# Up layers that run on unnormalised x, with 1/rms put in at the relu, and square sums moved to GpSimd

## The reference

```python
def rms_norm(x, g):
    xf = x.astype(jnp.float32)
    y = xf * lax.rsqrt(jnp.mean(xf * xf, axis=-1, keepdims=True) + NORM_EPS)
    return (y * g.astype(jnp.float32)).astype(x.dtype)

...
        x = x + jnp.concatenate([o_mix, o_mem], axis=-1) @ p['w_out'][i]
        h = rms_norm(x, p['norm_ffn_g'][i])
        x = x + jnp.square(jax.nn.relu(h @ p['w_up'][i])) @ p['w_down'][i]
    y = rms_norm(x, p['final_norm_g'])
```

## Time and profile before

| | us |
|---|---|
| median of 3 runs | 2136.28 |
| lowest, highest | 2129.35, 2141.01 |
| profiled execution | 2138.74 |
| its span | 2137.0 |
| TensorE busy | 2010.4 (94%) |
| VectorE busy | 1004.9 (47%) |
| ScalarE busy | 460.6 (22%) |
| GpSimd busy | 15.8 (1%) |
| mean granted clock of TensorE | 0.956 |

### The profile page before, as it was taken

The page is one execution under the profiler, slowest core; times in us unless marked ns, Lnnn a source line. Parts: engine busy times, 40 slices in busy tenths (PEclk is TensorE's granted clock), DMA queues, the critical chain, the costliest instruction groups (busy, mean ns, idle before and its releaser), DMA issues.

```text
span 2137.0 us, 26562 instructions
## 1 busy us (share of the span) xinstructions
PE 2010.4 (94%) x10334; PEld 1625.0 (76%) x10334; DVE 1004.9 (47%) x2078; ACT 460.6 (22%) x1179; POOL 15.8 (1%) x32
## 2 busy tenths in 40 slices
PE   8999888999979899999999999999989899999996
PEld 6888555677757788888887888788876688888885
DVE  3110799545554445355433424066545444445443
ACT  2211666333221111100001512233341111100000
POOL 0000000000000000000000000000000000000000
PEclk9999999999979899999999989999998999999998
DMA  5442100455522122222223111200001122222211
GB/s 217 165 150 73 40 1 1 139 178 177 158 79 79 60 79 79 79 79 89 89 72 150 60 40 60 82 32 1 31 28 60 59 79 79 81 89 87 79 60 42
DMA packets 60287, 175.41 MB, mean 82 GB/s; under 512 B 6529, under 2 KB 39442, under 8 KB 46850
## 3 DMA queue, kind: packets, MB, share of 16 engines
q1 hardware_dynamic: 56898, 160.77, 22.4%
q0 software_dynamic: 3264, 12.93, 1.5%
HBM read 160.75 MB, written 12.93 MB: 81 GB/s over the span
## 4 chain that ended last, share of the span: by engine, by line
PE 89%; DVE 6%; ACT 3%; issue 1%; DMA 0%; POOL 0%; SPq 0%; DVEq 0%; POOLq 0%; ACTq 0%
PE psum L1720 43%; PE psum L1704 15%; PE psum L842 5%; PE psum L1253 5%; PE psum L1686 2%; PE psum L915 2%; PE psum L698 2%; PE psum L679 1%; PE psum L875 1%; PE psum L1858 1%; PE psum L662 1%; DVE sbuf L1587 1%; DVE sbuf L789 1%; ACT sbuf L740 1%; PE psum L583 1%
## 5 line engine op out<-in xcount | busy, mean ns | idle before, releaser
L1720 PE MATMUL psum<-sbuf 128*128 128x272 f32 x4032 | 938.5, 395 | 24.6 <-DVE sbuf L2063 20.2
L1720 PEld LDWEIGHTS psum<-sbuf 128*128 128x128 f32 x4032 | 767.7, 191 | 193.6 <-DVE sbuf L2063 21.1
L1704 PE MATMUL psum<-sbuf 128*128 128x272 f32 x1344 | 329.4, 405 | 5.3 <-DVE sbuf L2063 5.3
L1704 PEld LDWEIGHTS psum<-sbuf 128*128 128x128 f32 x1344 | 261.1, 196 | 64.4 <-issue 6.7
L1923 ACT ACTIVATE sbuf<-sbuf 128x544 f32<-128x544 f32 x40 | 25.7, 655 | 545.0 <-DVE sbuf L2145 386.0
L1253 PE MATMUL psum<-sbuf 128*128 128x128 f32 (+3 forms) x1020 | 124.7, 278 | 12.4 <-DVE sbuf L1571 5.2
L1253 PEld LDWEIGHTS psum<-sbuf 128*128 128x128 f32 (+3 forms) x1020 | 117.6, 190 | 19.4 <-DVE sbuf L1571 6.0
L842 PE MATMUL psum<-sbuf 128*128 128x256 f32 x448 | 107.9, 392 | 0.0
L842 PEld LDWEIGHTS psum<-sbuf 128*128 128x128 f32 x448 | 82.0, 188 | 17.5 <-issue 1.2
L2074 DVE TENSOR_TENSOR sbuf<-sbuf 128x512 f32<-128x512 f32 x72 | 49.8, 691 | 86.8 <-PE psum L1720 86.7
L1948 ACT ACTIVATE sbuf<-psum 128x544 f32<-128x544 f32 x42 | 26.2, 623 | 293.2 <-PE psum L1704 293.2
(11 more groups left out here) (365 smaller groups left out, 2061.3 us busy)
## 6 DMA issues: line engine op xcount, KB each, us to landing
sbuf<-in_w SPq DMA_DIRECT2D x100, 1024.0 KB, 4.8
sbuf<-in_pages SPq DMA_DIRECT2D x256, 128.0 KB, 2.4
sbuf<-in_mcache SPq DMA_DIRECT2D x2, 4096.0 KB, 15.7
sbuf<-in_win SPq DMA_DIRECT2D x8, 512.0 KB, 4.6
out_win_o<-sbuf POOLq DMA_DIRECT2D x8, 512.0 KB, 2.9
sbuf<-in_state SPq DMA_DIRECT2D x6, 512.0 KB, 6.0
out_state_s<-sbuf POOLq DMA_DIRECT2D x6, 512.0 KB, 3.0
sbuf<-in_x SPq DMA_DIRECT2D x1, 2176.0 KB, 11.8
```

Of the source, the lines that this page charges most:

```text
L1704: last = mm(both(t % 2)[:, half, :], lhs, halves_of(rhs(k))[:, half, :], start=k == 0, stop=k == KT - 1)
L1720: ins = mm(to, lhs(k), rhs(k), start=first and k == 0, stop=last_ and k == 3, skip_group_check=True)
```

## The change

1. **Up on unnormalised x.** ScalarE copies x times the gain into a new buffer `xg`, block by block as VectorE finishes the blocks of each out unit (`gained`); up multiplies `xg`. The factor 1/rms is the same for all channels of a token, so it is put in after the product: VectorE's step is now max(c, 0) * rstd, and ScalarE squares the result. `xg` takes the place of the last 8 tiles of `u`, which move to `hT`.
2. **Squares.** ScalarE squares tile 0 into `sq_sum`, and GpSimd adds tiles 1 to 6 to it. TensorE sums only `sq_sum` and tile 7 (`norm_sums`): 4 matmuls for a norm instead of 16. For norms 1 and 3 they stand behind the first up unit, and the root and the reciprocal beside the second.
3. **Pairs.** The scheme now pairs tile 2k with 2k + 1 (before: k with k + 4), so the input sums of up can be made a pair at a time beside the out units (`gain_sums`).
4. **Order in a unit**: products 1, 5, 6, 2, 7, 3, 4 (before 1, 2, 6, 5, 7, 3, 4). The first unit of each out has 1, 2, 5, 6, 7, 3, 4.
5. **Heads of out.** For out0 the sums over the columns without samples, over the memory tiles, and the weight sums are made before the last sample is read. For out1 the weight sums are made before the last reciprocal of the mixer. TensorE no longer waits for the last read.
6. **Stores** of the result are issued by SyncE. Several semaphores are joined, and SyncE waits for norm 2's sums before it loads four tables of layer 1.

```diff
-        u = view(sbuf[:, pj0 + 8192 - FFT * TT_:pj0 + 8192], FFT, TT_)
+        u0 = pj0 + 8192 - FFT * TT_
+        u_low = view(sbuf[:, u0:u0 + 24 * TT_], 24, TT_)
+        xg = view(sbuf[:, u0 + 24 * TT_:u0 + FFT * TT_], KT, TT_)
+        u_at = lambda t, n: u_low[:, t:t + n, :] if t < 24 else hT[:, t - 24:t - 24 + n, :]
...
+        LATE, EARLY = (1, 5, 6, 2, 7, 3, 4), (1, 2, 5, 6, 7, 3, 4)
...
+                    sp.wait_ge(sq_used, KT + 2)
                     sp.dma_start(mkv[1], mem_out[1]).then_inc(in_mkv1, 16)
...
+            for k in range(KT):
+                sp.wait_ge(h_ready, 2 * KT + k + 1)
+                sp.dma_start(y_out[:, k, :], hT[:, k, :]).then_inc(y_stored, 16)
...
+            def add_squares(n):
+                for k in range(1, KT - 1):
+                    pool.wait_ge(sq_ready, n * KT + k + 1)
+                    if k > 1:
+                        pool.wait_ge(sq_added, 6 * (n - 1) + k - 1)
+                    pool.tensor_tensor(sq_sum, sq_sum, sq[:, k % 2, :], ALU.add).then_inc(sq_added, 1)
...
+            before_last()
             dve.wait_ge(cn_std, 2)
             dve.reciprocal(rinv[0:TS, 4, :], rinv[0:TS, 4, :]).then_inc(cn_rec, 1)
...
+            def norm_sums(n):
+                pe.wait_ge(sq_added, 6 * n)
+                for half in range(2):
+                    mm(both(3)[:, half, :], ones, halves_of(sq_sum)[:, half, :], start=True, stop=False)
+                pe.wait_ge(sq_ready, (n + 1) * KT)
+                for half in range(2):
+                    last = mm(both(3)[:, half, :], ones, halves_of(sq[:, 1, :])[:, half, :], start=False, stop=True)
+                last.then_inc(sq_used, 1)
...
             def up(l, n):
-                pe.wait_ge(h_ready, (n + 1) * KT)
                 for g in range(UP_U):
-                    strassen(ubase[f"up{l}"] + g, lambda k: hT[:, k, :], lambda k: hT[:, 4 + k, :], tsum[0],
-                             TSUM[f"up{l}"], 1)
+                    if g == 0:
+                        pe.wait_ge(gain_ready, 16 * (l + 1) - 1)
+                    strassen(ubase[f"up{l}"] + g, lambda k: xg[:, 2 * k, :], lambda k: xg[:, 2 * k + 1, :], tsum[0],
+                             TSUM[f"up{l}"])
+                    if g == 0:
+                        norm_sums(n)
...
+            def root(n):
+                act.wait_ge(sq_used, KT + n)
+                f(halves_of(rstd), both(3), ACT.Sqrt, bias=C["eps"], scale=1.0 / D).then_inc(std_ready, 1)
...
+            def square(n, k):
+                if k >= 3:
+                    act.wait_ge(sq_added, 6 * (n - 1) + k - 2)
+                f(sq[:, k % 2, :] if k else sq_sum, xT[:, k, :], ACT.Square).then_inc(sq_ready, 1)
...
+                for g in range(OUT_U):
+                    U, lo, hi = ubase[f"out{l}"] + g, 2 * g, 2 * g + 1
+                    act.wait_ge(*read_out(U, "c11"))
+                    f(xg[:, lo, left], xT[:, lo, left], ACT.Copy, scale=gain[:, lo:lo + 1]).then_inc(gain_ready, 1)
+                    act.wait_ge(*read_out(U, "u3"))
+                    f(xg[:, hi, right], xT[:, hi, right], ACT.Copy, scale=gain[:, hi:hi + 1]).then_inc(gain_ready, 1)
+                    act.wait_ge(*read_out(U, "c12"))
+                    f(xg[:, lo, right], xT[:, lo, right], ACT.Copy, scale=gain[:, lo:lo + 1]).then_inc(gain_ready, 1)
+                    square(n, lo)
+                    act.wait_ge(*read_out(U, "c21"))
+                    f(xg[:, hi, left], xT[:, hi, left], ACT.Copy, scale=gain[:, hi:hi + 1]).then_inc(gain_ready, 1)
+                    square(n, hi)
...
-                    c = u[:, 2 * g:2 * g + 2, :]
-                    stt(out=c, in0=c, scalar=0.0, in1=c, op0=ALU.max, op1=ALU.mult).then_inc(u_ready, 1)
+                    c = u_at(2 * g, 2)
+                    stt(out=c, in0=c, scalar=0.0, in1=rstd.unsqueeze(1).to_broadcast([P, 2, TT_]), op0=ALU.max,
+                        op1=ALU.mult).then_inc(relu_ready, 1)
...
+                    if g == 1:
+                        dve.wait_ge(std_ready, n + 1)
+                        own(dve.reciprocal(rstd, rstd))
```

More of the change, by code:

```diff
@@ L1929, in convolved, with down_squares @@
+            def down_squares(l, n):
+                for g in range(4):
+                    U = ubase[f"down{l}"] + 12 + g
+                    act.wait_ge(*read_out(U, "c12"))
+                    square(n, 2 * g)
+                    act.wait_ge(*read_out(U, "c21"))
+                    square(n, 2 * g + 1)
+                root(n)
             def convolved(t):
@@ L2033, in _ @@
             memory_norm()
-            norm(0)
+            first_norm()
             memory_kv()
@@ L2293, in _ @@
             gdn_steps()
-            dve_gdn(dve, own)
-            out("out1", gproj, XQ1)
-            norm(3, C["g_ffn"][:, 1, :])
+            dve_gdn(dve, own, before_out1)
+            dve.wait_ge(cn_ready, GH + 1)
+            memory_sums(44, tsum[1], gproj, XQ1)
+            mixed_sums(48, tsum[1], slice(0, HALF))
+            out(1)
             dve.wait_ge(stored, 32)
-            dve.wait_ge(state_stored, 16 * GH)
             up(1, 3)
```

410 lines of the change are left out of this document (224 added, 186 removed).

## The result

The changed kernel takes 2080.39 us (median of four runs, 2079.95 to 2087.12) where the kernel before took 2136.69 beside it: a ratio of 0.9747, with a 95% interval of 0.9714 to 0.9781. The forecast was 2087, with 2077 to 2100 as its range. The profiled execution of after took 2080.59 us, with a span of 2078.8, against the profiled span of 2137.0 before: 58.2 us less, where the sum had said 49.8. The question left is therefore where 8 us more came from, and whether the parts that seem to fit do so for the reasons given.

What follows compares the result with a forecast made beforehand. The prediction took TensorE's own work (busy 94%) as the bound, leaving only the seams to win. Its terms, 19.2 + 18.0 + 2 x 5.1 + 2.5 - 0.6 + 0.5 = 49.8 us, took the median 2136.28 to 2087 us, range 2077 to 2100.

Steps and rivals of the forecast that it cites:

- The seams: Passages from out to up: TensorE's pause and the lower clock behind it go, saving 19.2 and 18.0 us.
- rival 3: Out-to-up passage does not close, part or all of a 14 us pause staying: 2106 to 2120 us; chance 0.05.
- The cover for the moved norm: Root, reciprocal and relu run beside the second up unit, hidden, with 1.4 us spare before TensorE's seventh product.
- E: The end of the last out product, from which the forecast counted times in the out-to-up passage.
- Rival 1: Second up unit gives back 3 to 6 us per layer, or heads cost their far ends: 2092 to 2100; chance 0.15.
- The tails: End of down with its norm: 3.7 us of square sums gone plus root 1.4 us earlier, 5.1 us, twice.
- The head of out0: Start of the first out layer: sums made before the last samples are read let the third product follow at once, 2.5 us saved.
- rival 4: New product order makes TensorE wait in 72 units; slower by 0.5% at 0.84 us per unit; chance 0.03.
- The head of out1: Start of the second out layer: weight sums ahead of the small reciprocal delay the spreading matmuls, 0.6 us lost.
- The end: Result stores issued by SyncE instead of GpSimd: 0.5 us saved, with 0 and 1.5 as ends.

Runs made afterwards that it cites:

- norm_serial: Changed kernel with sums, root and reciprocal of norms 1 and 3 again ahead of up's first unit, TensorE waiting for the reciprocal: 2105.56 us, ratio 0.9862.
- lnexp: Changed kernel with root and reciprocal of norms 1 to 4 replaced by a logarithm and an exponential on ScalarE: 2078.07 us, ratio 0.9734.
- dve_adds: Changed kernel with the 24 additions of squares moved from GpSimd to VectorE: 2081.03 us, ratio 0.9752.
- late_sums: Changed kernel with all input and weight sums for out0 made after the last sample's read again: 2087.34 us, ratio 0.9783.
- recip_first: Changed kernel with the small reciprocal at the head of out1 put ahead of the four weight sums again: 2078.69 us, ratio 0.9736.
- second_early: Changed kernel with product order 1, 2, 5, 6, 7, 3, 4 in all units but the first of each up layer: 2144.22 us, ratio 1.0034.
- pool_stores: Changed kernel with the eight result stores issued by GpSimd again, behind its additions: 2084.13 us, ratio 0.9753.

## Why the prediction was right, and where it was off

**The seams (19.2 and 18.0) were right, and for the reason given.** The 31 products in 57.20 us leave no room for a pause, the granted clock stays at 1.00, and with the norm put ahead again (norm_serial) 17.4 us come back, with the lower clock behind each pause. From the fifth out product to the next norm's reciprocal the forecast had 24.3 and 23.1 us, seam and tail together; 23.7 and 22.4 were measured, 0.6 and 0.7 short. With 5.0 for each tail (below) that leaves 18.7 and 17.4 for the seams. One reading in rival 3 was off: its pause of 14 us begins with the last pair of square sums, 1.85 us, and TensorE was idle for 12.1 us. The sum does not use it.

**The cover for the moved norm held.** Forecast: root's end at E + 15.7, reciprocal's at + 19.3. With E = 693.67 + 0.92 - 14.7 = 679.9, the rows have the root's end at + 15.4 and the reciprocal's at + 19.0. TensorE's seventh product in that unit did not wait, and lnexp, which takes 1.6 us out of this chain (3.55 of reciprocal for 1.28 of table load and 0.66 of exponential), changed nothing there. Rival 1 is out.

**The tails (5.1 each) were right, with an addition that was priced too low.** GpSimd's addition took 1.16 us, not the 0.7 chosen. The forecast's estimate from the Trainium skill (GPSIMD Engine Reference, section 3.1 Elementwise) was 1.2 to 1.4, and this trace is just below that. The difference hardly shows. From the tail of down 0:

```profile
1092.85 1.14 POOL L550 TENSOR_TENSOR sbuf<-sbuf 128x544 f32<-128x544 f32 x1 [9.88 <-ACT sbuf L1975]
...
1093.95 0.66 ACT L1975 ACTIVATE sbuf<-sbuf 128x544 f32<-128x544 f32 x1 [1.18 <-DVE sbuf L2246]
1094.04 1.19 PE L1727 MATMUL psum<-sbuf 128*128 128x272 f32 x4 [0.60 <-POOL sbuf L550]
...
1096.18 0.71 ACT L1962 ACTIVATE sbuf<-psum,sbuf 128x544 f32<-128x544 f32 x1 [1.58 <-PE psum L1730]
```

The last product ends at 1093.45, the sixth addition at 1093.99 (+ 0.54), and TensorE waits 0.60 us for it; but the last square is done only at 1094.61, so the addition costs no more than what dve_adds showed, 0.3 us. The root starts at + 2.7; the forecast had + 2.6, and before it was + 4.03. With the two pairs of sums between the units, 3.7, that is 5.0.

**The head of out0 (2.5) was 0.9 too high.** The early sums gave their 2.0 us (late_sums). The forecast came down to 18.0 us from the last sample's group to the fifth product; after has 18.9. Some 0.25 of this is that the four products took 10.23 us and not 9.98, which moves with the clock (9.00 in recip_first). What was missed is in the order: the first out unit runs 1, 2, 5, 6, 7, so that product 6 stands directly ahead of 7 in the same bank, and TensorE waits 0.62 us before 7:

```profile
635.55 4.83 PE L1763 MATMUL psum<-sbuf 128*128 128x272 f32 x20 [0.62 <-DVE sbuf L2229]
```

The forecast had said, under rival 4, that two products on the same bank still have one of 1.84 us between them. That is so for 70 units and not for these two. second_early put the same neighbours into nearly all units and cost 62 us: rival 4's mechanism is real, at 0.86 us a unit, its threshold for "slower" of 0.84 was about right, and it is the late order that keeps it away. Its small chance was well judged only because the code of the other units does keep them apart; the sentence that gave the reason was too general.

**The head of out1 (-0.6) came out right, in part by luck**: -0.75. The delay is by the mechanism named: the first product starts 6.66 us after the last state addition, where the forecast has 6.7. Behind it two misses cancel: TensorE waits the same 0.6 us before product 7, and the four products took 9.79 us where the forecast's own terms give 10.26. recip_first takes the loss back with 1 us more. It was told too kindly: 1.74 us can be had by moving one line.

**The end (0.5, with 0 to 1.5 as its ends) was the mis-sized term.** 3.6 us were measured, and the queue accounts for all of it (3.56 in pool_stores). The rows at hand showed when the last issue was and how long it took, and the step that failed was to price the move by these alone. What follows an issue was in the profile of before as well: 15.6 us from the last reciprocal to the end of the span, of which reciprocal and scalings are 9.2.

**The rest, 7.7 us, was no term of the sum at all.** It lies in stages with the same code on TensorE. 5.9 of it is the gated delta input stage, where the time goes with the granted clock. recip_first shows that the change does not bring it by itself; what decides it stays open. Without it after would stand at about 2088, one microsecond from the forecast. So the measured time is better by something that the forecast could not see.

That the changed parts come to 50.6 us against 49.8 is partly luck as well: of the five rows of the table that it had priced, four came out below their terms, by 2.35 us together (0.9, 0.6, 0.15 and 0.7), and the end 3.1 above its own. The main mechanism, the seams, does not rest on this.

## What to carry to other kernels

Where a positive per-row factor commutes with the next matmul and its activation, run the matmul on the raw input and bring the factor in behind: the gain is the pause plus the lower clock that follows it. It held here, where the moved chain (5.6 us from the root to the end of the first relu) stood beside a unit of 12.86 us. When reordering accumulations over few PSUM banks, keep one product between two of the same bank (here 0.86 us per pair, 62 us by the medians, more than the whole change won). And at the end of a program look at which queue issues the last stores, and read the price from the last issue to the end of the span, not from the issue itself.

## What the hardware showed that was not expected

- Stages whose instructions on TensorE are identical differ by up to 7.5 us in 261 (253.6 to 261.2), and by up to 8 us in the attention stage (423.4 to 431.3). TensorE's mean granted clock goes with it: 0.97 to 0.94 in the first, 0.93 to 0.90 in the second. Differences of this size between kernels need a stage-by-stage reading before they are put down to an edit.
- Behind the last store issued by GpSimd the span goes on for 3.3 us after the last DMA is busy, behind SyncE's for 0.9 us, and a landing takes 3.0 us against 2.2.
- The logarithm and the exponential each loaded a table of their own, 1.28 us each; so the short way around a reciprocal of 3.55 us saves 1.6.
- A tensor addition on GpSimd took 1.16 us for 544 columns where VectorE took 0.73, and one of VectorE's that met it ended 0.3 us after it (1.04 us instead of 0.44).
